# Decoder step on one core: how the scaled token columns of the prompt blocks are made

## The reference, cut to what matters

```python
def rmsnorm(x, g):
    xf = x.astype(jnp.float32)
    y = xf * lax.rsqrt(jnp.mean(xf * xf, axis=-1, keepdims=True) + EPS) * g
    return y.astype(x.dtype)

def memory_kv(mem, norm_mem, w_ck, w_cv):          # 256 memory tokens
    hm = rmsnorm(mem, norm_mem)
    mk = (hm @ w_ck).reshape(bsz, n_mem, X_HEADS, X_HEAD_DIM)
    mv = (hm @ w_cv).reshape(bsz, n_mem, X_HEADS, X_HEAD_DIM)
    return mk, mv

def hybrid_layer(x, mem_k, mem_v, ...):
    h = rmsnorm(x, norm_mix)
    proj = h @ w_in                                 # then mixer, output projection
    ...
    x = x + jnp.concatenate([o_a, o_b], axis=-1) @ w_out
    ...                                             # then cross-attention, w_cq, w_co
```

## Time and profile before

| what | us |
|---|---|
| median of 3 runs | 1714.95 (1713.89 to 1715.65) |
| the profiled execution's own time | 1714.2 |
| its span in the trace | 1712.4 |
| PE busy in the span | 1684.6 (98%) |
| DVE, ACT, POOL busy | 770.1, 615.9, 153.8 |

### The profile page before, as it was taken

The page is one execution under the profiler, slowest core; times in us unless marked ns, Lnnn a source line. Parts: engine busy times, 40 slices in busy tenths (PEclk is TensorE's granted clock), DMA queues, the critical chain, the costliest instruction groups (busy, mean ns, idle before and its releaser), DMA issues.

```text
span 1712.4 us, 31645 instructions
## 1 busy us (share of the span) xinstructions
PE 1684.6 (98%) x13216; PEld 1560.6 (91%) x13216; DVE 770.1 (45%) x1301; ACT 615.9 (36%) x1008; POOL 153.8 (9%) x171
## 2 busy tenths in 40 slices
PE   6999999999999999999999999999999999999998
PEld 5887899999999999999999999999999986499998
DVE  5676437665756747646334343233121143422222
ACT  5555335344442543444222222223121133322232
POOL 0000001111121121111000001111000000000110
PEclk9999999999999999999999999999999999999999
DMA  7797643233332342432243235444432386733422
GB/s 258 238 295 229 211 107 104 73 98 100 79 89 59 104 109 55 113 99 76 73 109 77 81 113 151 119 144 129 153 95 78 122 345 250 223 94 97 122 82 105
DMA packets 272401, 225.18 MB, mean 131 GB/s; under 512 B 9801, under 2 KB 239058, under 8 KB 266850
## 3 DMA queue, kind: packets, MB, share of 16 engines
q1 hardware_dynamic: 272064, 223.96, 43.3%
q10 hardware_dynamic: 258, 0.09, 0.0%
HBM read 199.08 MB, written 25.30 MB: 131 GB/s over the span
## 4 chain that ended last, share of the span: by engine, by line
PE 95%; DVE 2%; issue 1%; DMA 1%; ACT 1%; POOL 0%; SPq 0%; DVEq 0%; ACTq 0%; POOLq 0%
PE pj L285 63%; PE pj L446 11%; PE pj L2547 2%; PE dk L2213 2%; PE pj L2234 1%; PE dk L365 1%; PE dk L2136 1%; PE pj L2147 1%; PE dk L1747 1%; PE pj L2243 1%; PE dk L1200 1%; PE dk L1206 1%; PE dk L752 1%; PE dk L2576 1%; DVE yq L914 1%
## 5 line engine op out<-in xcount | busy, mean ns | idle before, releaser
L285 PE MATMUL pj<-a_hi,w_high 128*128 128x272 f32 x2432 | 526.2, 298 | 0.0
L285 PE MATMUL pj<-a_hi,w_low 128*128 128x272 f32 x2432 | 502.9, 288 | 0.0
L285 PE MATMUL pj<-a_lo,w_high 128*128 128x272 f32 x2432 | 501.5, 288 | 0.0
L285 PEld LDWEIGHTS pj<-a_hi,w_high 128*128 128x128 f32 x2432 | 381.5, 189 | 13.2 <-issue 8.1
L269 DVE TENSOR_TENSOR w_low<-w_raw,w_high 128x2048 fp32r<-128x2048 f32 x96 | 219.8, 2289 | 368.5 <-ACT w_high L259 368.4
L285 PEld LDWEIGHTS pj<-a_lo,w_high 128*128 128x128 f32 x2432 | 382.2, 188 | 0.0
L285 PEld LDWEIGHTS pj<-a_hi,w_low 128*128 128x128 f32 x2432 | 379.9, 189 | 0.1
L259 ACT ACTIVATE w_high<-w_raw 128x2048 fp32r<-128x2048 f32 x96 | 183.4, 1910 | 49.8 <-PE pj L285 42.4
L285 PE MATMUL pj<-mix_hi,w_high 128*128 128x272 f32 x512 | 105.9, 288 | 0.0
L285 PE MATMUL pj<-mix_lo,w_high 128*128 128x272 f32 x512 | 105.5, 288 | 0.0
L285 PE MATMUL pj<-mix_hi,w_low 128*128 128x272 f32 x512 | 105.2, 287 | 0.0
(11 more groups left out here) (416 smaller groups left out, 2029.1 us busy)
## 6 DMA issues: line engine op xcount, KB each, us to landing
w_raw<-in_w_in_dram SPq DMA_DIRECT2D x48, 1024.0 KB, 6.1
w_raw_wide<-in_w_ck_dram SPq DMA_DIRECT2D x16, 1024.0 KB, 6.3
w_raw_wide<-in_w_cv_dram SPq DMA_DIRECT2D x16, 1024.0 KB, 5.6
w_raw<-in_w_out_dram SPq DMA_DIRECT2D x16, 1024.0 KB, 5.9
w_raw<-in_w_cq_dram SPq DMA_DIRECT2D x16, 1024.0 KB, 5.8
w_raw<-in_w_co_dram SPq DMA_DIRECT2D x16, 1024.0 KB, 6.1
xr<-xT_scratch SPq DMA_DIRECT2D x16, 272.0 KB, 6.2
x2T_scratch<-x SPq DMA_DIRECT2D x16, 272.0 KB, 5.3
```

The costliest lines, as they stand in the source:

```text
L285: mm = pe.matmul(pj[:, 2 * (q % 2) + b, 0:n], wt[:, k, :], x(k, o, n), start=(k == 0 and m == 0), stop=(k == KT - 1 and m == 2))
```

## The change

For the five token blocks only the raw rows are turned. The scaled columns are then made from the turned raw ones: DVE writes a matrix `diag` with the reciprocal roots on its diagonal, one product of a matrix of ones with it lays the row of roots across all partitions, DVE copies that to `rbc`, and POOL multiplies the four groups of `xts` by it into `xs_cols`. ACT and DVE then make high and low parts from `xs_cols` in SBUF instead of from PSUM. The squares of blocks 1 to 5 go to `xin[1]` as throw-away output. The raw turns stand at q = 0 and 1 after steps 2 and 9; the product of ones stands at q = 2 after step 4. SP's loads of the next block wait for `squared` in place of `x_scaled`. Later waits on `x_turned` 48 become waits on `x_bank` 53.

```diff
+        diag, rbc = take("diag", [P]), take("rbc", [P])
+        xs_cols = put("xs_cols", [KT, P], F32, M_W + 2 * D)
...
+        turned_before = lambda j: 8 + 5 * (j - 1)
+        banked_before = lambda j: 8 + 9 * (j - 1)
+        scaled_before = lambda j: 2 + 5 * (j - 1)
+        high_before = lambda j: 8 + 4 * (j - 1)
...
+        def x_root(dve, j, rows):
+            dve.wait_ge(rooted, j + 2)
+            dve.reciprocal(stat[0:rows, 2:3], stat[0:rows, 1:2]).then_inc(inverted, 1)
+            dve.wait_ge(inverted, j + 2)
+            dve.tensor_scalar(diag[0:rows, 0:rows], ident[0:rows, 0:rows], stat[0:rows, 2:3], None, ALU.mult).then_inc(x_scaled, 1)
+        def x_cols_high(act, j, b, rows):
+            act.wait_ge(x_scaled, scaled_before(j) + 2 + b)
+            for k in range(4 * b, 4 * b + 4):
+                a = act.activation(a_hi[:, k, j * P - P:j * P - P + rows], xs_cols[:, k, 0:rows], ACT.Copy,
+                                   scale=gain[:, G_MIX + k:G_MIX + k + 1])
+            a.then_inc(x_high, 1)
+        def x_cols_low(dve, j, b, rows):
+            dve.wait_ge(x_scaled, scaled_before(j) + 2 + b)
+            dve.wait_ge(x_high, high_before(j) + b + 1)
+            at = slice(j * P - P, j * P - P + rows)
+            for k in range(4 * b, 4 * b + 4):
+                a = dve.scalar_tensor_tensor(a_lo[:, k, at], xs_cols[:, k, 0:rows], gain[:, G_MIX + k:G_MIX + k + 1],
+                                             a_hi[:, k, at].bitcast(F32), ALU.mult, ALU.subtract)
+            a.then_inc(x_bank, 1)
+        def pool_mem(pool):
+            for j in range(1, 6):
+                rows = x_block(j)
+                pool.wait_ge(x_turned, turned_before(j))
+                pool.wait_ge(x_high, high_before(j))
+                pool.wait_ge(x_bank, banked_before(j) + 5)
+                for b in range(4):
+                    pool.tensor_tensor(xs_cols[:, 4 * b:4 * b + 4, 0:rows], xts[:, 4 * b:4 * b + 4, 0:rows],
+                                       rbc[:, 0:rows].unsqueeze(1).to_broadcast([P, 4, rows]), ALU.mult).then_inc(x_scaled, 1)
...
             def turn(j, b):
-                    if b == 4:
-                        pe.wait_ge(x_scaled, j + 2)
-                    x_turn(pe, xin[0] if b < 4 else xst, 8 * j + b, b + 2, b % 4, x_block(j))
+                    drained = banked_before(j) + b - 1 if b > 1 else 8 if j == 1 else banked_before(j - 1) + 5
+                    x_turn(pe, xin[0], drained, b % 3, b, x_block(j))
+            def spread_roots(j):
+                def step(pe):
+                    rows = x_block(j)
+                    pe.wait_ge(x_scaled, scaled_before(j) + 1)
+                    pe.wait_ge(x_bank, banked_before(j) + 2)
+                    pe.matmul(dk[:, 1, 0:rows], ones[0:rows, :], diag[0:rows, 0:rows], start=True, stop=True).then_inc(x_turned, 1)
...
                     if 1 <= j <= 5:
-                        steps = {3: [turn(j, 2 * q)], 9: [turn(j, 2 * q + 1)]}
+                        steps = ({2: [turn(j, 0)], 9: [turn(j, 1)]}, {2: [turn(j, 2)], 9: [turn(j, 3)]},
+                                 {4: [spread_roots(j)]}, {})[q]
...
                         if q == 1:
-                            x_scale(dve, j + 1, xin[0], rows)
+                            x_root(dve, j, rows)
+                        if q == 2:
+                            dve.wait_ge(x_turned, turned_before(j) + 5)
+                            dve.tensor_copy(rbc[:, 0:rows], dk[:, 1, 0:rows]).then_inc(x_bank, 1)
+                        if q > 1:
+                            for b in (2 * q - 4, 2 * q - 3):
+                                x_cols_low(dve, j, b, rows)
```

More of the change, by code:

```diff
@@ L329, in build @@
         MEM_GROUPS, KEY_GROUPS = 8, 4
-        def banks_before(n):
-            return 0 if n == 0 else 8 * (n - 1)
+        turned_before = lambda j: 8 + 5 * (j - 1)
+        banked_before = lambda j: 8 + 9 * (j - 1)
+        scaled_before = lambda j: 2 + 5 * (j - 1)
+        high_before = lambda j: 8 + 4 * (j - 1)
         def x_stats(act, n, src, rows):
@@ L340, in x_stats @@
                 act.wait_ge(x_loaded, 16 * max(n, 1))
-            xs, o = (xsm, 4) if n == 1 else (xst, 0)
-            if n != 1:
-                at_least(act, x_turned, banks_before(n))
+            xs, o = (xsm, 4) if n == 1 else (xst if n == 0 else xin[1], 0)
+            if n > 1:
+                act.wait_ge(x_scaled, 2)
             act.activation(xs[0:rows, :], src[0:rows, :], ACT.Square,
@@ L358, in x_scale, with x_turn @@
             dve.tensor_scalar(xs[0:rows, :], src[0:rows, :], stat[0:rows, o + 2:o + 3], None, ALU.mult).then_inc(x_scaled, 1)
-        def x_turn(pe, src, c, slot, part, rows):
-            at_least(pe, x_bank, c - 1)
+        def x_turn(pe, src, drained, slot, part, rows):
+            at_least(pe, x_bank, drained)
             for m in range(4):
@@ L411, in sp_mem @@
                         if j < 5:
-                            sp.wait_ge(x_scaled, j + 2)
-                            sp.wait_ge(x_turned, 8 * j + 4)
+                            sp.wait_ge(squared, j + 2)
+                            sp.wait_ge(x_turned, turned_before(j) + 4)
                             if j == 4:
@@ L417, in sp_mem @@
                                 sp.dma_start(xin[0][:], t["x_prompt"][0, j * P:j * P + P, :]).then_inc(x_loaded, 16)
-                        sp.wait_ge(x_bank, 8 * j + 4)
+                        sp.wait_ge(x_bank, banked_before(j) + 4)
                         sp.dma_start(xT_d[:, :, j * P - P:j * P - P + x_block(j)].rearrange("k p r -> p k r"),
@@ L421, in sp_mem @@
                     if q == 0 and j == 6:
-                        sp.wait_ge(x_scaled, 7)
-                        sp.wait_ge(x_turned, 44)
+                        sp.wait_ge(squared, 7)
+                        sp.wait_ge(x_turned, turned_before(6))
                         sp.dma_start(scrow[0:24, :], t["state_conv"].rearrange("o b j n -> (o b j) n")).then_inc(vec_loaded, 16)
@@ L465, in step @@
                         pe.wait_ge(x_scaled, c + 1)
-                    x_turn(pe, (xst, xsm)[c % 2], c, c, c // 2, P)
+                    x_turn(pe, (xst, xsm)[c % 2], c - 1, c, c // 2, P)
                 return step
@@ L473, in step @@
                         pe.wait_ge(x_loaded, 16 * (j + 1))
-                    if b == 4:
-                        pe.wait_ge(x_scaled, j + 2)
-                    x_turn(pe, xin[0] if b < 4 else xst, 8 * j + b, b + 2, b % 4, x_block(j))
+                    drained = banked_before(j) + b - 1 if b > 1 else 8 if j == 1 else banked_before(j - 1) + 5
+                    x_turn(pe, xin[0], drained, b % 3, b, x_block(j))
+                return step
+            def spread_roots(j):
[4 more added lines that the diff above has]
+                    pe.matmul(dk[:, 1, 0:rows], ones[0:rows, :], diag[0:rows, 0:rows], start=True, stop=True).then_inc(x_turned, 1)
                 return step
@@ L493, in turn_conv @@
                 pe.wait_ge(vec_loaded, 16 * 8)
-                pe.wait_ge(x_bank, 48)
+                pe.wait_ge(x_bank, banked_before(6))
                 for k in range(NQKV):
@@ L562, in act_mem @@
                     if 1 <= j <= 5 and q > 1:
-                        for b in (2 * q, 2 * q + 1):
-                            x_take_high(act, 8 * j + b, b + 2, b % 4, a_hi, j * P - P, x_block(j), G_MIX)
+                        for b in (2 * q - 4, 2 * q - 3):
+                            x_cols_high(act, j, b, x_block(j))
         def dve_mem(dve):
@@ L591, in dve_mem @@
                         rows = x_block(j)
[L592 to L600, removed]
-                        if q == 1:
-                            x_scale(dve, j + 1, xin[0], rows)
+                        for b in (2 * q, 2 * q + 1) if q < 2 else ():
+                            dve.wait_ge(x_turned, turned_before(j) + b + 1)
+                            if b == 0:
+                                at_least(dve, xts_stored, 16 * (j - 1))
+                                dve.wait_ge(x_scaled, scaled_before(j))
+                            dve.tensor_copy(xts[:, 4 * b:4 * b + 4, 0:rows],
+                                            dk[:, b % 3, 0:4 * rows].rearrange("p (m r) -> p m r", m=4)).then_inc(x_bank, 1)
+                        if q == 1:
+                            x_root(dve, j, rows)
[3 more added lines that the diff above has]
+                        if q > 1:
+                            for b in (2 * q - 4, 2 * q - 3):
+                                x_cols_low(dve, j, b, rows)
                     if j == 7 and q == 1:
@@ L723, in sp_rows @@
             if q is None:
-                sp.wait_ge(x_turned, 48)
+                sp.wait_ge(x_bank, banked_before(6))
                 sp.wait_ge(xts_stored, 80)
@@ L735, in pool_rows @@
         def pool_rows(pool):
-            pool.wait_ge(x_turned, 48)
+            pool.wait_ge(x_bank, banked_before(6))
             pool.wait_ge(vec_turned, 2)
@@ L2633, in _ @@
```

(1 more changed line is left out.)

## The result

The changed kernel takes 1704.59 us (median of 5, 1704.16 to 1705.00) against 1714.42 of the kernel before, run beside it (median of 5; the 1714.95 known ahead was the median of its first three). The ratio is 0.9942, 95% interval 0.9929 to 0.9955: faster by 9.8 us, where 8.45 (1714.95 - 1706.5) was forecast. The predicted 1706.5 was 1.9 us too high, and 1704.59 lies 0.2 us under the stated range. Of the 1.9 us, 0.5 is the starting value (1714.95 against 1714.42) and 1.4 is that the kernel gained more than the sum says.

A forecast was written before the change was run, and what follows sets the result against it. PE was taken to bound the mem stage; 9.76 us removed less 1.25 added gives 8.5, so 1714.2 - 8.5 = 1705.7, and 0.75 us for the median makes 1706.5. The range was 1704.8 to 1709.9.

The forecast's parts named there:

- What bounds the kernel: Mem stage: PE is gapless, so each microsecond of PE work removed comes off the end if others deliver in time.
- The net of 8.5 us for the stage: Mem stage: 9.76 us of removed turns less 1.25 us of new products, ends 7.3 and 8.7.
- The removed turns: PE, five blocks: sixteen groups at 0.47 us and four at 0.56, together 9.76 us.
- The five products: PE, one fp32 product of ones per block: 0.25 us each, 1.25 in all, ends 1.1 and 2.45.
- Do the others keep up: DVE, ACT and POOL in one block: no PE wait; narrowest, one microsecond to spare at the xts copy before the third turns.
- The slope: Raising POOL's multiply time x moves both ACT chains by 2x: xts copy late from 1.75 us, cast from 2.0.
- The Trainium skill's GPSIMD Engine Reference, section Key points: POOL beside DVE's low parts: POOL's last two results up to 1.13 us later each, without PE waiting.
- Transfers at nothing: Full groups: 7.34 million bytes at 293 GB/s instead of 275, with no cost in time.
- Rival A: POOL and DVE slow each other, POOL to 2.0 us: 2 us lost over four blocks, 1708.5; chance 0.10.
- B: Transfers bound the four full groups: 6.5 us lost, only the last block's 1.95 stay, 1713.0; chance 0.05.
- C: POOL at 3.2 us per repeated-operand multiply: 18.4 us lost, 1724.9; decides at about 2.5 us per multiply; chance 0.03.
- the half microsecond allowed for later stages: After the mem stage: half a microsecond for a different starting phase, lowering the range's lower end from 1705.3 to 1704.8.

The follow-up runs named there:

- the two runs: Changed kernel with each POOL multiply preceded by one like it into a spare tile, 1721.08 us, or by one of 256 elements, 1713.24 us.
- product_four: Changed kernel with the product of ones made four times in a row in each block, fifteen products more: 1709.57 us, ratio 0.9974 to the kernel before.
- the kernel before is filled: Kernel before with nine unread matmuls of 256 columns ahead of each of PE's last two waits: 1713.44 us, ratio 0.9998.

## Why the prediction was right and where it failed

- What bounds the kernel: right. PE is gapless in the same stretch, and the turns put back without any reader bring their time back. The signs named for this came too: a period of 24.98 us, products of 0.22, POOL's multiplies at 1.29, and ACT's cast at q = 3 (90.00) 2.2 us behind the tile's start.
- The net of 8.5 us for the stage: right, measured 8.50, but luck has a part in the hundredths. The removed turns were put at 9.76 us from periods and cost about 9.9 (9.5 by putting them back, and the 0.43 of the wait that went away with it). The five products were put at 1.25 and cost 1.0, at 0.20 each. The wait of the third group of turns was put at nothing and cost 0.43. Together 9.9 - 1.0 - 0.4 is 8.5 again. A group's own row of 0.36 to 0.44 would have given too little, the period did not.
- Do the others keep up: nearly, but the room was not there. One microsecond was laid out at the third group of turns, and the trace has it waiting by 0.1. Four low parts that took 1.13 are held by POOL: the eight of q = 2 end about 11.5 us into the tile, not at 9.5. High parts from SBUF take 389 ns each in place of 370. The rest of the chain then moves by less, since DVE already had to wait for ACT's cast. The slope was wrong too: ACT's fourth group waits for POOL's fourth result, so from there on a slower POOL counts four times, not twice (by the two runs 8.6 us for 0.54 us more of POOL in four blocks, 4.0 a block), and the split of the group's first tile is a third wait that I had not priced.
- The Trainium skill's GPSIMD Engine Reference, section Key points: the contention with DVE instructions that have two SBUF inputs is here. I let it delay POOL. In the changed mem stage POOL always begins first, so POOL kept 1.30 us (mean of 16: 1304 ns; 1291 where no low part ran beside it) and DVE paid, up to 1.39 us for an instruction of 0.34 and 1.9 us for a block. I had also misread: in the slow ones of 1.63 to 1.66 us it is not DVE's split of weights that runs beside POOL but its low part (L1853), begun 0.34 to 0.38 us earlier.
- Transfers at nothing: right. At 309 GB/s no cast of the stage waits for a load.
- Rival A had the right pair of engines and the wrong one waiting; its 2.0 us for POOL, when tried, cost 8.0 us where 2 stood. B did not come (its last block is 1.99 us by the sum's own terms, not 1.95; nothing hangs on it). C named the cast and the `xts` copy, and both did block; at 2.5 to 2.6 us for a multiply it cost 16.7 us and the kernel was slower than before, so it decides already near 2.0 (1713.24 us), not at 2.5.
- The step that failed is the last, "It ran 0.75 us under the median shown, so the median comes to 1706.5", together with the half microsecond allowed for later stages. The median shown was of three runs. Over the four jobs it was 1714.2 to 1714.4, as the profiled execution's 1714.2 had it, so the 0.75 us had no ground; without it the forecast is 1705.7, 1.1 us above the measured time. That rest is late: behind the mem stage the two traces differ by 1.35 us, not by half a microsecond at most.
- Of the late part, 0.4 to 0.5 us are in the last group, in every trace, cause open. The other place is the tail, up to 1 us where the long fall of the clock is missing. That the long fall belongs to the execution and not to one kernel's code is shown by the trace of product_four, and its price by the tails: 14.8 to 15.1 us with it, 13.9 when the kernel before is filled. Three of the four unfilled traces of the old code had it and one of eight of the new. The clocks of all executions (57 of 108 at 0.998 or less against 22 of 54) lean the same way, but not clear of chance. Whether the change makes the fall rarer stays open.

## What to carry to other kernels

Price PE work from periods of the steady state, with and without it: here that gave the turns to 0.2 us of 9.9. Ahead of a forecast take the scatter of the runs as its own term, since a median of three was 0.5 to 0.7 us off, and look at the granted clock of the tail. When POOL gets work beside DVE, look which of the two begins first, and price a DVE instruction with two SBUF inputs as one that may have to wait out POOL's, and the other way round; keep POOL's instructions short or DVE's order away from them. A net sum that fits to the hundredth doesn't show that its terms do.

## What the runs showed of the hardware

- A scalar_tensor_tensor of DVE with both tensor inputs in SBUF takes 0.34 us alone and up to 1.39 us when it begins while POOL's tensor_tensor of 1.3 us is under way; POOL takes 1.29 to 1.34. A tensor_tensor of DVE on other tiles does the same (1.45 us, kernel before, 368.10). Begun 0.34 us ahead of POOL's, DVE's keeps its 0.78 us, and POOL's takes 1.66; begun 0.6 us ahead, 1.37 to 1.43.
- A multiply of POOL over 512 elements takes 1.29 us with one operand of 128 elements repeated four times, as with plain operands (1.30).
- With two idle stretches of PE of about 1.45 us each at the end, the granted clock fell to 0.50 for about 3.4 us in six traces and 6.8 in four, and stayed at 1.00 to the last turn in two. With eighteen unread matmuls in them it stayed at 1.00 in all three. The tail is 1 us longer at 6.8 us and the same within 0.3 at 3.4, where the stores end last.
